# Gate weights of a merge stage split in two parts, and a third of one modulation's rows moved to the input stages

## The reference

```
h  = rms_norm(x, norm_g[0]) * (1 + sc1) + sh1
u  = h @ w_in                                   # u_gate is its last 4*2048 columns
gates = sigmoid(u_gate).reshape(b, l, 4, 2048)
m  = sum_i gates[:, :, i] * branches[i]         # branches[i] = (branch i) @ its own output weights
y  = m @ w_o
x  = x + g1 * rms_norm(y, norm_g[1])            # and so on: the MLP, then the second block
```

## Time and profile before

| | us |
|---|---|
| median of 3 runs | 4039.57 |
| lowest, highest | 4029.41, 4048.44 |
| the profiled execution's own time | 4033.3 |
| its span (first to last instruction) | 4031.6 |

### The profile page before, as it was taken

The page is one execution under the profiler, slowest core; times in us unless marked ns, Lnnn a source line. Parts: engine busy times, 40 slices in busy tenths (PEclk is TensorE's granted clock), DMA queues, the critical chain, the costliest instruction groups (busy, mean ns, idle before and its releaser), DMA issues. The chain is left out here.

```text
span 4031.6 us, 53593 instructions
## 1 busy us (share of the span) xinstructions
PE 3758.7 (93%) x20888; PEld 3144.1 (78%) x20888; DVE 2113.4 (52%) x3104; ACT 1122.3 (28%) x1425; POOL 232.7 (6%) x276
## 2 busy tenths in 40 slices
PE   8998978968888899999989999999897999999998
PEld 5785465458888888888778888888787778888887
DVE  0171564654333345445566565555546476566565
ACT  1201021032222100000244343343433344344343
POOL 0000000112232200000000000000000000000000
PEclk9899989978879899999999999999997999999999
DMA  8553642700000298888535555555352345555553
GB/s 326 209 187 105 229 157 104 283 31 1 1 1 1 96 352 330 334 343 320 180 131 185 182 185 185 188 185 184 122 187 73 125 146 187 185 186 186 185 184 137
DMA packets 94465, 697.40 MB, mean 173 GB/s; under 512 B 10480, under 2 KB 10480, under 8 KB 13296
## 3 DMA queue, kind: packets, MB, share of 16 engines
q1 hardware_dynamic: 70272, 516.78, 36.1%
q0 software_dynamic: 23040, 167.78, 11.1%
q10 hardware_dynamic: 1008, 10.75, 0.6%
HBM read 693.17 MB, written 2.10 MB: 172 GB/s over the span
## 5 line engine op out<-in xcount | busy, mean ns | idle before, releaser
L1936 PE MATMUL ps<-hT_parts,rows_parts 128*128 128x512 f32 x3300 | 1178.7, 398 | 0.0
L1935 PE MATMUL ps<-hT_parts,ring_parts 128*128 128x256 f32 x3300 | 934.9, 283 | 3.2 <-DVE hT_parts L1886 3.2
L455 PE MATMUL ps<-hT,ring 128*128 128x256 f32 (+1 forms) x3520 | 910.7, 421 | 26.5 <-ACT work L700 10.5
L1908 DVE TENSOR_TENSOR ring_parts<-ring,rows_parts 128x2048 fp32r<-128x2048 f32 (+1 forms) x332 | 751.8, 2266 | 294.4 <-ACT rows_parts L1903 293.9
L455 PEld LDWEIGHTS ps<-hT,ring 128*128 128x128 f32 x3520 | 674.6, 192 | 259.8 <-issue 174.9
L1903 ACT ACTIVATE rows_parts<-ring 128x2048 fp32r<-128x2048 f32 (+1 forms) x332 | 628.1, 1892 | 387.6 <-DMA ring<-in_mlp_u 218.8
L1936 PEld LDWEIGHTS ps<-hT_parts,rows_parts 128*128 128x128 f32 x3300 | 625.1, 189 | 137.7
L1935 PEld LDWEIGHTS ps<-hT_parts,ring_parts 128*128 128x128 f32 x3300 | 625.9, 190 | 24.7 <-DVE hT_parts L1886 14.9
L1936 PE MATMUL ps<-work_parts,rows_parts 128*128 128x512 f32 x1616 | 575.8, 398 | 0.0
L335 DVE CUSTOM_DVE_ANT_0 rows<-rows 128x2048 f32<-128x2048 f32 x160 | 366.5, 2291 | 273.2 <-DMA rows<-in_ada_r 234.9
L1935 PE MATMUL ps<-work_parts,ring_parts 128*128 128x256 f32 x1616 | 451.8, 280 | 0.0
(11 more groups left out here) (392 smaller groups left out, 3376.4 us busy)
## 6 DMA issues: line engine op xcount, KB each, us to landing
ring<-in_mlp_u SPq DMA_DIRECT2D x128, 1024.0 KB, 4.9
rows<-in_ada_r POOLq DMA_DIRECT2D x96, 1024.0 KB, 7.7
ring<-in_ffn_u SPq DMA_DIRECT2D x88, 1024.0 KB, 4.9
rows<-in_mod_r POOLq DMA_DIRECT2D x64, 1024.0 KB, 5.4
ring<-in_gate_u SPq DMA_DIRECT2D x64, 1024.0 KB, 7.7
ring<-in_in_u SPq DMA_DIRECT2D x36, 1024.0 KB, 4.9
ring<-in_mod_u SPq DMA_DIRECT2D x32, 1024.0 KB, 4.9
ring<-in_down_u SPq DMA_DIRECT2D x32, 1024.0 KB, 4.9
```

The lines of the kernel that those rows point to most:

```text
L455: mm = pe.matmul(outs[o], wtile(u + o, kt), rhs(kt), start=kt == 0, stop=kt == KT - 1)
L1908: dve.tensor_tensor(ring_parts[:, u % SLOTS, 0:size], slot(u)[:, 0:size], w_high[:, u % SLOTS, 0:size].bitcast(F32), ALU.subtract)\
L1935: pe.matmul(ps[:, b, low_half], low, top(kt), start=False, stop=False)
L1936: mm = pe.matmul(ps[:, b, :], high, both(kt), start=False, stop=kt == kts - 1)
```

## The change

Merge: each gate unit is rounded by ACT (`round_unit`) and its remainder taken by DVE (`rest_unit`). PE makes three accumulating products of 256 columns for each 128x128 tile, instead of one float32 product. The input h is split too, once, by ACT and DVE, before the first product. RwOut's pieces are placed inside Merge: its transposes behind the first two units on PE, its last ACT and DVE steps behind the first sigmoid and the fourth remainder. The rounded weights lie in four places (`unit_high`). There is one buffer for the branches' weights (`bo_buf`) and one for the gates instead of two each. The loops of Merge are written out. The second load of x moves from SP at the head of Merge to POOL at its end.

Modulation: 32 of the 96 `ada` rows are fetched and multiplied in SsdIn and RwIn (`EARLY = 32`); Merge has 64 columns, one behind each remainder. Lines of the new kernel are named with their own numbers in the order listings only.

```diff
-        def fetch_rows(pool, src, first, n):
+        EARLY = 32
+        def fetch_rows(pool, src, first, n, at=0):
...
                 fetch_rows(pool, mod_r, 0, ADA0)
+                fetch_rows(pool, ada_r, ADA0, EARLY)
...
-                    first_columns(dve, 2 if n < 8 else 1)
+                    first_columns(dve, 4 if n < 8 else 1)
...
-                    first_columns(dve, 1 if n < 2 else 3 if n < 6 else 0)
+                    first_columns(dve, 2 if n < 2 else 4 if n < 6 else 0)
...
         class Merge:
             def sync(sp):
+                for p in range(PAIRS2):
+                    for b in range(4):
+                        for o in range(2):
+                            u = merge_unit(p, b, o)
+                            sp.wait_ge(w_used, u - SLOTS + 1)
+                            sp.dma_start(slot(u), gate_u[u - seg_merge]).then_inc(w_ready[u % SLOTS], 16)
+                        if b == 1:
+                            if p:
+                                sp.wait_ge(bk.full[6], use_bo[3][1] + p)
+                            else:
                                 sp.wait_ge(rw_ready, RT)
-                                if jj == 0:
-                                    sp.dma_start(xT[:, :, :], x_t).then_inc(x_in, 16)
...
             def tensor(pe, own):
-                            gemm_pair(pe, seg_merge + 2 * n, main_rhs, pair(n % 2), [(n % 2, use_gate[n % 2][1] + n // 2)], it=it, k=4, step=16)
...
+                            pe.wait_ge(w_split, u - SPLIT0 + 1)
+                            for kt in range(KT):
+                                if u == seg_merge and kt % 4 == 0:
+                                    pe.wait_ge(h_split, kt // 4 + 1)
...
+                                high, low = unit_high(u)[:, columns], ring_parts[:, u % SLOTS, columns]
...
+                                pe.matmul(out, high, h_high[:, kt, :], start=kt == 0, stop=False)
+                                pe.matmul(out, high, h_low[:, kt, :], start=False, stop=False)
+                                mm = pe.matmul(out, low, h_high[:, kt, :], start=False, stop=kt == KT - 1)
...
+                        if p == 0 and b == 0:
+                            RwOut.tensor(pe, own)
...
             def scalar(act, own):
...
+                round_unit(act, seg_merge)
+                for n in range(0, KT, 4):
+                    act.activation(h_high[:, n:n + 4, :], hT[:, n:n + 4, 0:T], ACT.Copy).then_inc(h_hi, 1)
+                for n in range(1, AHEAD_ACT):
+                    round_unit(act, seg_merge + n)
+                RwOut.scalar_root(act, own)
+                for p in range(PAIRS2):
+                    act.wait_ge(merged, p)
+                    for b in range(4):
+                        for o in range(2):
...
+                            if u == seg_merge + 1:
+                                continue
+                            if u + AHEAD_ACT < MERGE_END:
+                                round_unit(act, u + AHEAD_ACT)
+                        unit_done(act, merge_unit(p, b, 1))
+                        emptied(gate_use(p, b), act.activation(gates[:, b, :], ps[:, b % 2, :], ACT.Sigmoid))
+                        if p == 0 and b == 0:
+                            RwOut.scalar_out(act, own)
+                            act.wait_ge(rw_ready, RT)
+                            round_unit(act, seg_merge + 1 + AHEAD_ACT)
...
             def gpsimd(pool, own):
-                fetch_rows(pool, ada_r, ADA0, 96)
+                fetch_rows(pool, ada_r, ADA0 + EARLY, 96 - EARLY, EARLY)
+                pool.wait_ge(w_used, MERGE_END)
+                pool.dma_start(xT[:, :, :], x_t).then_inc(x_again, 16)
...
             def vector(dve, own):
-                        for n in range(12):
-                            column(dve, adaT, vec("ada_b"), 1, ADA0 + 12 * jj + n, 12 * jj + n, it, 24)
...
+                RwOut.vector_sums(dve, own)
+                rest_unit(dve, seg_merge)
+                for n in range(0, KT, 4):
...
+                    dve.tensor_tensor(h_low[:, n:n + 4, :], hT[:, n:n + 4, 0:T], h_high[:, n:n + 4, :].bitcast(F32), ALU.subtract).then_inc(h_split, 1)
+                for n in range(1, AHEAD_DVE):
+                    rest_unit(dve, seg_merge + n)
+                RwOut.vector_scaled(dve, own)
...
+                for p in range(PAIRS2):
+                    for b in range(4):
+                        for o in range(2):
+                            u = merge_unit(p, b, o) + AHEAD_DVE
+                            if u == seg_merge + 1 + AHEAD_ACT:
+                                RwOut.vector_out(dve, own)
+                            if u < MERGE_END:
+                                rest_unit(dve, u)
+                            i = EARLY + 8 * p + 2 * b + o
+                            column(dve, adaT, vec("ada_b"), 1, ADA0 + i, i)
```

More of the change, by code:

```diff
@@ L342, in first_columns @@
         def first_columns(dve, n):
-            for i in range(columns_done[0], min(columns_done[0] + n, ADA0)):
-                column(dve, modx, vec("mod_b", 32, 96), 0, i, i)
-            columns_done[0] = min(columns_done[0] + n, ADA0)
+            for i in range(columns_done[0], columns_done[0] + n):
+                if i < ADA0:
+                    column(dve, modx, vec("mod_b", 32, 96), 0, i, i)
+                else:
+                    column(dve, adaT, vec("ada_b"), 1, i, i - ADA0)
+            columns_done[0] += n
         class Mod:
@@ L1727, in branch_kernel @@
         seg_merge = segment(8 * PAIRS2)
-        bo_buf = [w(W0 + n * BO_K * 2 * P, BO_K * 2 * P, k=BO_K) for n in range(2)]
-        gates = [w(W0 + 2 * BO_K * 2 * P + n * 8 * T, 8 * T, b=4) for n in range(2)]
+        MERGE_END = seg_merge + 8 * PAIRS2
+        bo_buf = w(W0, BO_K * 2 * P, k=BO_K)
+        gates = w(W0 + BO_K * 2 * P, 8 * T, b=4)
+        M0 = W0 + BO_K * 2 * P + 8 * T
+        m_all = w(M0, KT * T, a=KT)
+        H0 = M0 + KT * T
+        assert H0 + UNIT <= WORK
         use_gate = [bk.take(b, 2 * PAIRS2) for b in range(2)]
@@ L1782, in scalar @@
-            def scalar(act, own):
-                act.wait_ge(rw_ready, RT)
-                with act.Fori(0, PAIRS2 // 2) as it:
-                    for jj in range(2):
-                        act.wait_ge(merged, it * 2 + (jj + 1))
-                        for b in range(4):
-                            n = 4 * jj + b
-                            unit_done(act, seg_merge + 2 * n + 1, it, 16)
-                            act.activation(gates[jj][:, b, :], ps[:, n % 2, :], ACT.Sigmoid).then_inc(bk.free[n % 2], 1)
+                            sp.dma_start(bo_buf.rearrange("p k n -> p (k n)"), bo_u[p]).then_inc(bo_ready, 16)
@@ L2002, in vector @@
             def vector(dve, own):
-                dve.wait_ge(merged, 2 + PAIRS2)
+                dve.wait_ge(merged, PAIRS2)
                 for n in range(AHEAD_DVE):
                     rest_unit(dve, seg_wo + n)
-                split_x(dve, own, hT[:, :, T:], h_low, h_high)
+                split_x(dve, own, m_all, h_low, h_high)
                 with dve.Fori(0, KT // 4) as it:
@@ L2655, in _ @@
                 RwScan.tensor(pe, own)
-                RwOut.tensor(pe, own)
                 Merge.tensor(pe, own)
@@ L2674, in _ @@
                 RwScan.scalar(act, own)
-                RwOut.scalar(act, own)
                 Merge.scalar(act, own)
@@ L2693, in _ @@
                 RwScan.vector(dve, own)
-                RwOut.vector(dve, own)
                 Merge.vector(dve, own)
```

148 lines of the change are left out of this document (82 added, 66 removed).

## The result

The changed kernel takes 4050.32 us (median of 20 runs, 4035.0 to 4076.61), the kernel before, timed beside it, 4033.2 (20 runs, 4023.03 to 4049.53). The ratio is 1.0035 with a 95% interval of 1.002 to 1.005: a little slower. The profiled execution of the changed kernel took 4067.13, its span is 4065.4.

A forecast was written before the change was run, and what follows sets the result against it. PE was taken to bound the kernel, busy 93% of the span, with DVE's waits for rows in the input stages. From 4033.3, Merge -67 and input stages +59 gave 4025; with the runs' median, 4029 was taken, range 3990 to 4068.

The forecast's parts named there:

- first pair: Merge's head: slow first units and a wait at the fifth gate unit make the first pair lose 4.3 us.
- The fifth unit: Merge's first pair: this gate unit's DMA stands behind SP's wait and the branch weights, so PE waits 10 us.
- The cover of 2.5 us: Merge's steady part: a gate unit's DMA starts 16.9 us ahead, needs 14.5, about 2.5 spare; costed at no wait.
- the mean round: Input stages: two columns per 8.62 us, the mean of twelve intervals with DVE waiting; SsdIn +38, RwIn +21.
- the stated bound of 10.65: Input stages: at the worst round, 10.65 us, SsdIn +77 and RwIn +52.
- rival 2: Merge becomes bound by transfers at 322 GB/s, PE waiting 6 us a pair: +42, time 4067 to 4073; chance 0.19.
- The lower bound: Input stages: at 8.05 us a round, SsdIn +32 and RwIn +13, together +45.
- rival 1: Input stages: rows keep better pace, rounds of 8.1 or less; at 8.05 net -22, 4011 to 4017; chance 0.28.
- 7.4 a round: Input stages: round by the Trainium skill's DMA formula; they would cost about 28 us, time near 3995.
- Rivals 3 and 4: Merge: weight loads not hidden, 4367; or PE's unit not shortened, waiting on ACT or DVE, 4092; chance 0.05 together.
- rival 3: Merge: loads of weights are not hidden under products, 1024 tiles take 275 us longer than before, time 4367.

The follow-up runs named there:

- the order experiment: Changed kernel with SsdIn's columns between the five taps of the convolution and RwIn's between the three steps of the shift; ratio to the kernel before 1.0024.
- The run with both edits: Changed kernel with columns between the taps and shift steps, and SsdIn's and RwIn's ring units bringing an eighth of their bytes; ratio to the kernel before 0.9978.
- split_96_spread: Changed kernel with all 96 ada columns in Merge, one behind each remainder and one ahead of each branch multiplication; ratio to the kernel before 0.9970.

## Why the prediction was wrong

**Merge: right.** Forecast 5.63 a gate unit, 60.6 a pair, first pair +4.3, -67 in all; measured 5.73, 61.19, +4.3 and -63. The 0.6 per pair is products that start 0.119 apart instead of 0.117. The loads of weights stayed hidden, as the rows of Mix had it. The fifth unit waited 10.9 (forecast 10) for its DMA behind SP's wait; the run with the branch weights later took that wait away. The cover of 2.5 us in the steady part held.

**The 32 rows: right mechanism, wrong size, and that turned the sign.** The step that failed is "I take the mean round, since a ring unit crosses the rows every 14 us as it did there", with 8.62. Measured 9.53 in SsdIn's tiles, 8.98 over RwIn's 31 intervals: +53 and +29 instead of +38 and +21. With small ring units the two stages cost 33 and 22, 55 together, near the forecast's 59: a mean that was meant to hold the crossings has the size of one nearly without them (8.54).

Why it came out so low can be seen in the trace of before. Averaged were the rounds in which DVE was seen to wait for the second row; up to 807.02 there are twelve, and their mean by the rows is 8.58, not 8.62, and with the thirteenth, the 10.65, 8.74. When a column is late, the row behind it is often in time, so the long round that ends there shows no wait and was left out. Yet to count all rounds would have been wrong too. All 22 from 704.39 to 814.14 have a mean of 9.54, but in that stretch DVE waits three times for ACT, which waits for PE, 6.4 us in all. The first time:

```profile
726.36 2.29 DVE L335 CUSTOM_DVE_ANT_0 rows<-rows 128x2048 f32<-128x2048 f32 x1 [3.27 <-DMA rows<-in_mod_r]
...
731.04 0.69 DVE L1180 TENSOR_TENSOR work<-work 128x512 f32<-128x512 f32 x1 [2.19 <-ACT work L1124]
...
733.16 2.28 DVE L335 CUSTOM_DVE_ANT_0 rows<-rows 128x2048 f32<-128x2048 f32 x1
```

The columns behind the three waits stand at 733.16, 761.94 and 790.73: PE gives two tiles with their six columns per 28.8 us, and that makes 9.6 a round whatever the rows do. That this is near the 9.53 of SsdIn later is chance. The 16 rounds that hold no wait for ACT have a mean of 8.94, and RwIn in the changed kernel, where PE seldom sets the pace, has 8.98. With 8.94 the prediction's own sum would have been +44 and +26, and 3 above the kernel before instead of 8 below. That is still 9 short in SsdIn. There the convolution, 4.1 long with its gaps, doesn't lie wholly inside a wait as the sum assumes (4.4 at most by the order experiment); the rest isn't attributed.

The 9.53 was inside the stated bound of 10.65, and the sentence under rival 2 ("Rounds of 9.3 and over in the input stages (+80 and more)", near 4050) had the right time. The lower bound was added up wrongly. At 8.05 a round the prediction's own terms give 395.73 + 9 x 16.1 + 12.95 + 28.4 = 582.0 for SsdIn, +27 and not +32; so 40 in all, and -27 instead of -22 for rival 1, and at 7.4 a round 18 instead of 28. The run with both edits, nearly at the bare round, has 582.9.

**The sum.** Forecast -67 + 59 = -8; measured in the profiles -63 + 83 = +20, and in the medians +17. RwScan's +15 in the profiled pair is the spread between executions.

**Rival 1** (better pace) is excluded: the means are 9.53 and 8.98, and no round is under 7.9 in the input stages of any run with full rows. **Rival 2** (Merge bound by transfers) didn't occur at 64 columns, 313 GB/s. At 96 columns PE did wait behind late columns, as it describes; that the loss is 6 per pair there, the rival's price for 64, is chance. Its 322 GB/s was no limit: that stage was held by PE, and moved 396 for 45 us. **Rivals 3 and 4** are excluded by 5.73 per unit. The rule of the Trainium skill ("TensorE: Matmul & The Clock Gate", section "The mechanism") behind rival 3, that a load of weights overlaps running products only when the row groups differ, would have added some 275 us by the prediction's price of a load. The trace disagrees again, with 5.73 for 48 products that each load weights.

What stays open: what decides whether RwScan gets a granted clock of 0.85, 0.83 or 0.81. The profiles show that no edit of this study decides it, not what does.

## What to carry to other kernels

Take the pace of a stream from all its intervals, not from those in which a wait for it is recorded: that choice drops long ones. But first take out those in which its reader waited for something else, or the mean is the pace of that (here 8.58 by the recorded waits, 9.54 over all, 8.94 without the waits for ACT, and 8.98 came). Work that is free under one bottleneck costs its full round of buffers elsewhere; look for gaps in which its engine, the DMAs and the engine that it shares a port with are all idle, and put it there. The same 32 rows cost 83 us in the input stages, 48 left in Merge, 35 to 52 in RwScan beside GpSimd's products, and nothing that can be seen in the gaps.

## What the runs showed of the hardware

- A DVE instruction with two SBUF inputs and a GpSimd instruction exclude each other. Here GpSimd's 1.27 us product took 1.78 on the mean and 3.39 at most in RwScan, where a column of 2.29 took up to 3.35; GpSimd's busy time there rose from 148 to 196 us for 32 columns. The Trainium skill ("SBUF — State Buffer", section "SBUF: two separate sides") calls the shared port pair an exclusive lock held for a whole instruction; the trace agrees. GpSimd's issues of row DMAs took 0.53 us in this run, and 0.67 at most.
- A row of 1 MB alone landed in 5.1 us in both input stages. Of the 60 rows that DVE waited for there in the changed kernel, 31 were read within 5.5 us of their DMA's issue, 13 within 7.0, and 16 after 7.4 to 10.05. With ring units of an eighth the mean in SsdIn falls from 6.4 to 5.4.
- PE's split products start 0.12 us apart at a granted clock of 1.00 (2.4 GHz). Behind each of PE's waits of 9 to 11 us in Merge they start 0.21 apart for 3 to 5 us, at a granted clock of 0.50 to 0.61; behind three waits of 1.5 us nothing of the kind shows (`split_96_spread`).
- One program's RwScan, 3976 records of PE, takes 512 or 529 us, at a granted clock of 0.85 or 0.81, in two executions of the same kernel. A change under 0.5% here needs the stages' marks, or many runs.
